# Experts of a two-block network: 256 gathers of key and value rows against panels of all keys and all values

## The reference

```python
def one_chunk(xt):                      # D = 1024, 8 heads, 128 x 128 = 16384 experts, top 16
    q = (xt @ w_q).reshape(BLOCK, PEER_HEADS, PEER_QDIM)
    s1 = jnp.einsum('chd,nd->chn', q[..., :half], keys1)
    s2 = jnp.einsum('chd,nd->chn', q[..., half:], keys2)
    t1, i1 = lax.top_k(s1, PEER_TOPK)
    t2, i2 = lax.top_k(s2, PEER_TOPK)
    cand = (t1[..., :, None] + t2[..., None, :]).reshape(BLOCK, PEER_HEADS, PEER_TOPK * PEER_TOPK)
    cidx = (i1[..., :, None] * PEER_NKEYS + i2[..., None, :]).reshape(...)
    ts, sel = lax.top_k(cand, PEER_TOPK)
    idx = jnp.take_along_axis(cidx, sel, axis=-1)
    g = jax.nn.softmax(ts, axis=-1)
    act = jax.nn.gelu(jnp.einsum('chkd,cd->chk', u[idx], xt))
    coef = (g * act).astype(xt.dtype)
    return jnp.einsum('chk,chkd->cd', coef, v[idx])
```

## Time and profile before

| | |
|---|---|
| time, median of 3 runs | 1437.83 us (1436.86 to 1438.47) |
| span of the profiled execution | 1437.5 us |
| PE busy | 1289.3 us, 90% of the span |
| DVE busy | 848.4 us, 59% |
| ACT busy | 422.1 us, 29% |
| POOL busy | 292.7 us, 20% |
| moved by DMA | 368 MB, a mean of 256 GB/s |
| mean granted clock of PE | 0.985 of full |

### The profile page before, as it was taken

One profiled execution on the slowest core, in us unless ns is written; L12 is line 12 of the kernel. 1 busy time (PEld: TensorE's weight loads), 2 busy tenths in 40 slices (PEclk: granted clock), 3 DMA queues, 4 the chain that ended last, 5 costly groups with the idle time before them and its releaser, 6 DMA issues.

```text
span 1437.5 us, 19206 instructions
## 1 busy us (share of the span) xinstructions
PE 1289.3 (90%) x7268; PEld 833.1 (58%) x7268; DVE 848.4 (59%) x2097; ACT 422.1 (29%) x974; POOL 292.7 (20%) x269
## 2 busy tenths in 40 slices
PE   7999998999999999999999989999877777777776
PEld 4446788986579878887888544444333332333322
DVE  7527866546563247232115867777777777777654
ACT  1215223121351136453003243333322322223212
POOL 0000000000000100000003344456543444444420
PEclk9999999999999999999999999999999999999999
DMA  9444100343324344432457999999999999999994
GB/s 308 158 151 133 33 3 3 118 146 117 118 89 151 110 136 148 127 106 88 146 209 297 421 421 403 421 421 421 421 421 421 421 421 420 422 421 420 422 422 202
DMA packets 68972, 367.98 MB, mean 256 GB/s; under 512 B 9295, under 2 KB 12751, under 8 KB 35793
## 3 DMA queue, kind: packets, MB, share of 16 engines
q0 software_dynamic: 37152, 269.50, 45.3%
q1 hardware_dynamic: 31586, 96.99, 20.4%
q10 hardware_dynamic: 144, 0.26, 0.0%
HBM read 365.67 MB, written 1.06 MB: 255 GB/s over the span
## 4 chain that ended last, share of the span: by engine, by line
PE 55%; DMA 24%; DVE 7%; ACT 2%; issue 1%; DVEq 0%; ACTq 0%
PE bank L1845 16%; PE bank L2491 11%; DMA arena<-peer_in,arena 7%; DMA row<-peer_in,arena 7%; DMA cst<-peer_in,arena 7%; PE bank L2437 3%; PE bank L1383 3%; DMA res<-peer_in,arena 2%; PE bank L1463 2%; PE bank L1440 2%; PE bank L805 2%; PE bank L614 1%; PE bank L604 1%; PE bank L1515 1%; PE bank L2425 1%
## 5 line engine op out<-in xcount | busy, mean ns | idle before, releaser
L2491 PE MATMUL bank<-arena 128*128 128x512 f32 x584 | 276.7, 614 | 65.1 <-ACT arena L2595 65.1
L2491 PEld LDWEIGHTS bank<-arena 128*128 128x128 f32 x584 | 109.1, 194 | 218.2 <-issue 217.9
L1845 PE MATMUL bank<-arena,ring 128*128 128x256 f32 (+2 forms) x1104 | 232.3, 371 | 2.2 <-DVE arena L2266 1.4
L1845 PEld LDWEIGHTS bank<-arena,ring 128*128 128x128 f32 x1104 | 198.8, 190 | 32.0 <-DVE arena L2266 1.8
L2732 DVE CUSTOM_DVE_ANT_0 arena<-arena 128x1024 f32<-128x1024 f32 x146 | 176.8, 1222 | 54.6 <-DMA arena<-peer_in,arena 54.4
L2777 POOL DMA_INDIRECT arena<-peer_in,arena x146 | 167.3, 1146 | 183.5 <-PE bank L2491 162.0
L2595 ACT ACTIVATE arena<-cst,arena 128x128 f32<-128x128 f32 x256 | 88.9, 394 | 133.8 <-DVE arena L2681 132.5
L2587 ACT ACTIVATE arena<-arena 128x2 f32<-128x2 f32 x129 | 38.0, 295 | 261.6 <-DVE arena L2732 261.5
L2491 PE MATMUL bank<-ring,arena 128*128 128x512 f32 x160 | 76.7, 623 | 21.7 <-ACT arena L2595 21.6
L2777 POOL DMA_INDIRECT row<-peer_in,arena x18 | 19.3, 1072 | 312.5 <-DVE arena L2669 276.3
L2491 PE MATMUL bank<-cst,arena 128*128 128x512 f32 x140 | 68.7, 624 | 13.6 <-ACT arena L2595 13.5
(11 more groups left out here) (400 smaller groups left out, 1982.1 us busy)
## 6 DMA issues: line engine op xcount, KB each, us to landing
ring<-stream_in SPq DMA_DIRECT2D x155, 512.0 KB, 3.6
ring<-stream_in SPq DMA_DIRECT2D x8, 384.0 KB, 6.5
arena<-stream_in SPq DMA_DIRECT2D x6, 512.0 KB, 7.2
arena<-peer_in,arena POOLq DMA_INDIRECT x146, 33.4
row<-rows_in SPq DMA_DIRECT2D x4, 512.0 KB, 18.7
cst<-cst_in SPq DMA_DIRECT2D x1, 1868.0 KB, 18.5
row<-rows_in POOLq DMA_DIRECT2D x2, 512.0 KB, 6.3
cst<-rg_w_in SPq DMA_DIRECT2D x1, 1024.0 KB, 7.9
```

The lines of the kernel that those rows point to most:

```text
L1845: mm = nc.tensor.matmul(bank[:, first:first + width], slot[:, at + k * cols:at + (k + 1) * cols], src[:, k, :], start=k == 0, stop=k == kt ...
L2491: mm = nc.tensor.matmul(core.banks[2 * t + b][:, :], diag[i % ND], value_half(i, b), start=False, stop=last)
```

## The change

No expert is gathered any more. The arrays u and v are brought in whole, as 128 panels each: panel j of the keys (`pu`) holds the experts whose second digit is j, 128 x 1024, and so does panel j of the values (`pv`). They come through the ring of `load_weights`, which has 4 places from then on instead of 8; the ring now takes panels in the order in which PE asks for them, and all transfers of SP are written at the end of the program.

PE meets all keys with all 256 normed tokens (`meet_keys`, 8 matmuls of 256 columns a panel). ACT takes the gelu of each pair of panels (`open_pair`) into an array G of 128 experts x 128 panels x 256 tokens. The routing stays on DVE, with its last steps on POOL (`decode`). PE turns the digits and weights so that choices lie on the partitions (`turn_picks`). For each token, POOL makes a matrix of 128 choices x 128 first digits that holds the weight where the digit fits (`make_ones`), DVE one of 128 choices x 128 second digits that holds ones, four tokens at once (`weigh_ones`), and PE multiplies the two: 128 x 128 weights for one token (`spread`, a group is four tokens, 64 groups). DVE multiplies these into the part of G that is there (`weave`), ACT copies the rest into G's part that is not there yet (`copy_rest`), and POOL multiplies the gelu of later panels onto it (`meet`). The spreads lie between the pairs of keys from pair 40 of 64 on, two or three groups after each pair. Then PE meets all values with G (`meet_values`, four matmuls of 512 columns a panel). The last projection of `second_mix` is made for 256 tokens at once there.

```diff
@@ -40,9 +40,7 @@
 DECAY = -float(np.exp(-0.5))
 SLOT = 1024
 RING = 8
-FIRST = 2
-EARLY = 7
-FIRST_AT = 17152
+LATE_RING = 4
...
-    out += [(("wq", m), SLOT) for m in range(EARLY, 2 * HP)]
+    out += [(("wq", m), SLOT) for m in range(2 * HP)]
+    out += [((name, j), D) for name in ("pu", "pv") for j in range(NK)]
...
+        elif key[0] == "pu":
+            m = tiles(w["peer_u_2"][0].reshape(NK, NK, D)[:, key[1]].T)
+        elif key[0] == "pv":
+            m = w["peer_v_2"][0].reshape(NK, NK, D)[:, key[1]]
...
+        if key not in self.slot_no:
+            place = self.next_place
+            self.next_place = (place + 1) % self.ring_places
+            self.place_count[place] += 1
+            self.came_before[key], self.in_place[place] = self.in_place[place], key
+            self.slot_no[key], self.slot_at[key] = len(self.slots), (place, self.place_count[place])
+            self.slots.append(key)
+        place, count = self.slot_at[key]
+        pe.wait_ge(self.slot_loaded[place], 16 * count)
+        return self.ring[place]
+    def shrink_ring(self):
+        self.ring_places, self.next_place = LATE_RING, 0
...
-            bank = claim(pe, ("mix", 0, m))
-            panel("mix", m, tiles(Y, T)[:, :, 0:P], KT, P, bank=bank).then_inc(*full(("mix", 0, m)))
+            panel("mix", m, tiles(Y, T), KT, T).then_inc(*full(("mix", m)))
+            core.used_by(("mix", m), ("mix", m))
...
+    UNITS = [(h, t) for h in range(HP) for t in range(TT)]
+    N, PAIRS = len(UNITS), NK // 2
+    QUAD, GROUPS, HELD = 4, T // 4, 3
+    WEAVE, LAST = 40, 4
...
+    def done_by(p):
+        return 0 if p < WEAVE else -(-(p + 1 - WEAVE) * GROUPS // (PAIRS - WEAVE))
+    def groups(p):
+        return range(done_by(p - 1), done_by(p))
+    pair_of = {q: p for p in range(PAIRS) for q in groups(p)}
...
+        def query(h):
+            key = ("wq", h)
+            bank = claim(pe, key)
+            for i in range(2):
+                slot = core.weights(pe, ("wq", 2 * h + i))
+                for k in range(KT):
+                    if h == 0 and i == 0:
+                        pe.wait_ge(g.gained.handle, k + 1)
+                    mm = nc.tensor.matmul(bank[:, i * T:(i + 1) * T], slot[:, k * P:(k + 1) * P], n2[:, k, :], start=k == 0, stop=k == KT - 1)
+                if i:
+                    mm.then_inc(*full(key))
+                    core.used_by(("wq", 2 * h + i), key)
+                else:
+                    mm.then_inc(*core.used_now(("wq", 2 * h + i)))
...
+        def meet_keys(j):
+            key = ("u", j // 2)
+            bank = core.banks[core.bank_at[key][0]] if j % 2 else claim(pe, key, 4 + j // 2 % 2)
+            slot = core.weights(pe, ("pu", j))
+            for k in range(KT):
+                mm = nc.tensor.matmul(bank[:, j % 2 * T:(j % 2 + 1) * T], slot[:, k * P:(k + 1) * P], normal[:, k, :], start=k == 0, stop=k == KT - 1)
+            if j % 2:
+                mm.then_inc(*full(key))
+                core.used_by(("pu", j), key)
+            else:
+                mm.then_inc(*core.used_now(("pu", j)))
...
+        def turn_picks(t):
+            key = ("picks", t)
+            bank = claim(pe, key, 6 + t)
+            pe.wait_ge(decoded.handle, N)
+            for i in range(2):
+                nc.tensor.transpose(bank[:, i * P:(i + 1) * P], index[:, i, t * P:(t + 1) * P], cst("ident"))
+            pe.wait_ge(weighed.handle, t + 1)
+            nc.tensor.transpose(bank[:, 2 * P:3 * P], weight[:, t * P:(t + 1) * P], cst("ident")).then_inc(*full(key))
...
+        def spread(q):
+            key = ("spread", q)
+            bank = claim(pe, key, 6 + q % 2)
+            pe.wait_ge(ones_weighed.handle, q + 1)
+            pe.wait_ge(ones_made.handle, q + 1)
+            for i in range(QUAD):
+                mm = nc.tensor.matmul(bank[:, i * NK:(i + 1) * NK], ONES[q % HELD][:, i, 0, :], ONES[q % HELD][:, i, 1, :], start=True, stop=True)
...
+        def meet_values(j, t):
+            slot = core.weights(pe, ("pv", j))
+            for b in range(2):
+                mm = nc.tensor.matmul(core.banks[2 * t + b][:, :], G[:, j, t * P:(t + 1) * P], half(slot, b), start=False, stop=j == NK - 1)
+                if j == NK - 1:
+                    mm.then_inc(*summed.up())
+            if t == TT - 1 and j < NK - 1:
+                mm.then_inc(*core.used_now(("pv", j)))
...
+        query(0)
+        core.shrink_ring()
+        g.ring_last = core.in_place[LATE_RING:]
+        sum_squares()
...
+        for h in range(2, HP):
+            query(h)
+            scores(h - 1)
+            if h == 2:
+                turn_factor()
+        scores(HP - 1)
+        pe.wait_ge(normed.handle, 1)
+        for p in range(PAIRS):
+            if p == WEAVE:
+                for t in range(TT):
+                    turn_picks(t)
+            for j in (2 * p, 2 * p + 1):
+                meet_keys(j)
+            for q in groups(p):
+                spread(q)
+        pe.wait_ge(woven.handle, GROUPS // 2)
+        for j in range(LAST):
+            meet_values(j, 0)
+        pe.wait_ge(woven.handle, GROUPS)
+        for j in range(LAST):
+            meet_values(j, 1)
+        pe.wait_ge(met.handle, PAIRS - WEAVE - 1)
+        for j in range(LAST, NK - LAST):
+            for t in range(TT):
+                meet_values(j, t)
...
-                for part in parts(n, q):
-                    act.wait_ge(dotted.handle, part.stop)
-                    nc.scalar.activation(act_out[:, part], dots[:, part], ACT.Gelu_apprx_tanh, scale=rstd[:, t:t + 1])\
-                      .then_inc(*activated.up())
-                    if q == 0 and 2 < n + 2 < N:
-                        scores(n + 2)
-                    act.wait_ge(coef_ready.handle, activated.count)
-                    for i in range(part.start, part.stop):
-                        if i >= ND:
-                            act.wait_ge(used.handle, i - ND + 1)
-                        nc.scalar.activation(diag[i % ND], cst("ident"), ACT.Copy, scale=act_out[:, i:i + 1])\
-                          .then_inc(*diag_ready.up())
...
+        def open_pair(p):
+            bank = filled(act, ("u", p))
+            before = done_by(p - 1) * QUAD
+            halves = tiles(bank[:, :], T)
+            if before:
+                n = p - WEAVE - 1
+                if n >= 2:
+                    act.wait_ge(met.handle, n - 1)
+                if n == 0:
+                    for key in g.ring_last:
+                        act.wait_ge(*core.slot_freed[key])
+                ins = nc.scalar.activation(tiles(spare[n % 2], T)[:, :, 0:before], halves[:, :, 0:before], ACT.Gelu_apprx_tanh)
+                ins.then_inc(*set_aside.up())
+            if before < T:
+                nc.scalar.activation(G[:, 2 * p:2 * p + 2, before:], halves[:, :, before:], ACT.Gelu_apprx_tanh).then_inc(*opened.up())
+                act.wait_ge(opened.handle, p + 1)
+            else:
+                act.wait_ge(set_aside.handle, set_aside.count)
+            act.sem_inc(*free(("u", p)))
+        def copy_rest(q):
+            bank = filled(act, ("spread", q))
+            first = 2 * (pair_of[q] + 1)
+            if first < NK:
+                by_key = bank[:, :].rearrange("p (t j) -> p j t", t=QUAD)
+                nc.scalar.activation(G[:, first:, tokens_of(q)], by_key[:, first:, :], ACT.Copy).then_inc(*rest_copied.up())
...
+        def weigh_ones(q):
+            if q < HELD:
+                for key in g.ring_last:
+                    dve.wait_ge(*core.slot_freed[key])
+            else:
+                filled(dve, ("spread", q - HELD))
+            copied(dve, ("picks", q * QUAD // P))
+            dve.wait_ge(laid.handle, q * QUAD // P + 1)
+            nc.vector.tensor_tensor(ONES[q % HELD][:, :, 1, :], index_t[:, tokens_of(q), 1:2].to_broadcast([P, QUAD, NK]),
+                                    cst("iota").unsqueeze(1).to_broadcast([P, QUAD, NK]), ALU.is_equal).then_inc(*ones_weighed.up())
+        def weave(q):
+            key = ("spread", q)
+            p = pair_of[q]
+            dve.wait_ge(opened.handle, min(p + 1, opened.count))
+            if rest_copied.count > q:
+                dve.wait_ge(rest_copied.handle, q + 1)
+            bank = filled(dve, key)
+            at = G[:, 0:2 * (p + 1), tokens_of(q)]
+            by_key = bank[:, :].rearrange("p (t j) -> p j t", t=QUAD)
+            nc.vector.tensor_tensor(at, at, by_key[:, 0:2 * (p + 1), :], ALU.mult).then_inc(*woven.up())
+            dve.wait_ge(woven.handle, q + 1)
+            dve.sem_inc(*free(key))
...
-                    for i in range(part.start, part.stop):
-                        arrived(dve, i)
-                        row = key_half(i)
-                        ins = nc.vector.tensor_tensor_reduce(out=row, in0=row, in1=half(X2, t), scale=1.0, scalar=0.0,
-                                                             op0=ALU.mult, op1=ALU.add, accum_out=dots[:, i:i + 1])
```

(50 more changed lines are left out.)

607 lines of the change are left out of this document (217 added, 390 removed).

## The result

The changed kernel takes 1805.67 us (median of 3, 1805.3 to 1808.13) against 1437.83 us before: 1.256 times as long, 95% interval 1.252 to 1.259. The profiled execution has a span of 1803.7 us; its own time is 1805.67 us. Every time given is the median of a kernel's fast runs: a single run of a single kernel, `e6_single_pass32` at 1455.05 us, was in the chip's slower state and is left out.

The account below looks back on a forecast made before the run. Gathers were taken to bound the experts stage before, PE the kernel after. From 737.5 us, 1039 us of PE work, 5.3 us to the end and 24 us of stall gave 1806 us (+25.6%), range 1780 to 1850.

Parts of the forecast that it names:

- The base: Start of the sum: PE's first matmul after the mixed rows, at 737.5 us.
- The 99 us of projection, queries and scores: PE work ahead of the keys, from last projection to turned picks: together 99 us.
- The keys: PE meeting 128 key panels: 2048 records of 256 columns at 0.216 us, 442 us.
- The values: PE meeting 128 value panels: 1024 records of 512 columns, 440 us, the same as the gathered form.
- The spreads and the stall: Weave, pairs 40 to 63: 58 us of outer products, plus PE idling about 1.5 us in 16 three-group pairs, 24 us.
- POOL's row: Weave: a weighted one-hot row of 128 columns takes POOL 0.22 us; POOL becomes the bound only at 0.8 us.
- POOL busy under a third: Sign expected in the profile after: POOL busy less than a third of the weave.
- rival (b): Weave worse through slow strided forms, slow POOL rows or a falling clock: 1851 us, or 1930 us; chance 0.25.
- The rule on the shared ports: Weave: one-hot blocks of DVE and POOL would alternate, 3 to 11 us more in all; left out of the sum.
- (c): Panel matmuls take one clock per column: 661 us go, end at 1145 us; chance 0.01.
- (a): Weave: the third group doesn't stall PE, 1782 us; chance 0.13.
- The claim on before: Experts stage of the kernel before: gathers bound it, 268 MB at 421 GB/s, 638 of 686 us.

Follow-up runs that it names:

- e6_single_pass32: Changed kernel with keys and values panels multiplied in float32r, panels rounded in place by ACT and DVE, and spreads begun at pair 32 instead of 40: 1444.68 us.
- e7_no_dve_ones: Changed kernel with DVE making its plain one-hot blocks for the first three groups only, 61 of 64 left out: 1793.87 us.
- e4_half_values: Changed kernel with values met for the first 512 of 1024 columns only, except in the last panel; all panels still brought in: 1595.16 us.
- e1_weave32: Changed kernel with spreads begun at pair 32 instead of 40, two groups in each of 32 pairs: 1782.67 us.
- e3_pool_half: Changed kernel with POOL making only two of the four one-hot rows of each group: 1801.88 us.
- e2_weave48: Changed kernel with spreads begun at pair 48 instead of 40, four groups in each of 16 pairs: 1846.15 us.
- b1_narrow_gathers: Kernel before, gathering 4 KB rows instead of 8 KB, keys alone, with the same number of gathers, rows and matmuls: 1357.9 us.
- e9_ring8_row4: As e8_ring8, with the fourth of each group's weighted one-hot rows made by DVE instead of POOL: 1309.44 us.
- e8_ring8: As e6_single_pass32, with eight ring places until three pairs before the spreads and again for the values: 1344.91 us.

## Why the prediction was right, point by point

**The base.** PE's first record of the projection started at 734.9 us, not 737.5. The two traces run within 0.2 us of each other for the first 150 us; from 120 to 240 us the mean clock was 0.97 before and 1.00 after, and the other kernels' traces have 736.1, 736.5, 737.1 and 737.2 there. The kernel after had gained its 2.5 us by 250 us, and from 160 to 200 us its mean granted clock was 1.00 and that of the others 0.87 to 0.96. But `e7_no_dve_ones` had 0.91 there and starts at 734.97 us, so the clock isn't all of it: it is scatter between executions of the same instructions, not the change.

**The 99 us of projection, queries and scores.** The first key panel starts at 832.37 us, 97.4 us on, and the picks, which the 99 us include, are turned in 0.65 us ahead of pair 40: six records, where I had counted twelve.

**The keys.** 442 us said. By starts the 80 panels before the weave took 276.3 us and each of the 24 pairs in it 6.91 us at the full clock, 442 us in all. The group's busy time is 448.1 us because the end of each row of records reaches 0.16 us into the first spread, and because of the low clock at 1121 to 1128 us. No idle time stands before it.

**The values.** 440 us said, 439.6 measured, and `e4_half_values` shows that they are worth that. This term carried the forecast: the dense form of the values costs PE what the gathered form did, so the keys and the spreads come on top.

**The spreads and the stall.** The values start at 1358.90 us, where I had 1360. PE idled 19.8 us, of which 15.5 behind DVE, 14 times at 1.1 us; I had 16 times 1.5. The chain was shorter by 0.4 us than I had it: the third group's spreads start 3.04 us after the first's, where I had 3.3, because ACT's two instructions for the pair overlap (0.66 us for both, not 0.77) and the hops are shorter, and PE's two spreads end at 1.95 us, not 1.8. That the weave cost nearly the 24 us anyway is luck: over its keys and spreads at full pace it took 26 us more, 19.8 of them idle, the rest the low clock after the wait for POOL and the ends of rows of records that idle time lays bare, neither of which is in my sum. The mechanism, the third block after the first weave, is shown three times: by `e1_weave32`, where it has no place, by `e3_pool_half`, where it stays with half of POOL's rows gone, and by `e7_no_dve_ones`, where the block isn't made. Strided reads of banks cost nothing extra: 0.52 us for 352 columns and 0.69 for 512 are the prices of the contiguous rows 7.

**What was mis-sized: POOL's row.** I took 0.22 us for a weighted one-hot row from a copy and a fill; it is 0.79 us by the median and 0.85 by the mean, about four times as much. The nearest rows, a fill and a copy, compare and multiply nothing, and said too little about it. I had put the point from which POOL decides at 0.8 us, and "POOL busy under a third" was wrong: it is busy 229 of 252 us. By my own threshold POOL would have been the bound. It cost 3.1 us of waits, 5 us with the clock behind them (`e3_pool_half`), because PE's pair with its stall took 10.2 us in the mean (10.9 us with three groups, from 1151.80 to 1162.72 us, and 8.7 with two), and POOL needed 10.7 x 0.85 + 0.7 = 9.8 us. The forecast was right here by 0.4 us a pair, which is luck. `e2_weave48`, with four groups a pair, shows what stands on the other side: 40 us more, with POOL as the bound and a low clock, which is rival (b)'s mechanism. The time that (b) gives for POOL at 1.5 us a row is wrong as it stands: 24 x 6.3 = 151 us come on top of 1806, 1957 us and not 1930.

**The rule on the shared ports.** The Trainium skill (SBUF — State Buffer, section "SBUF: two separate sides") has a DVE instruction with two SBUF inputs and a POOL instruction that reads SBUF block each other for a whole instruction. The runs agree that the two slow each other: with DVE's blocks POOL's rows take 852 ns, without them 799, and only rows that overlap a block are slow. They don't show a full block. In the changed kernel a row of POOL ran from 1153.74 to 1154.53 us and took 0.79 us as ever, while DVE's block of 1154.05 us took its 0.69 us; the next row took 0.90. In the mean a block of 0.69 us cost POOL 0.25 us ((939 - 790) x 107 / 64 ns), and apart from the very first row none took over 1.35 us. The price was on POOL, which had just room for it, and not 3 to 11 us on PE: DVE's blocks took 0.69 us by the median and 0.72 by the mean.

**The rivals.** (c) falls for float32: 2048 records of 216 ns for 1024 matmuls. For float32r it nearly is what happens: one record a matmul, 12 to 17% above one clock a column. (a) fell: the stall is there. That the transfers are hidden held: no wait of PE for a panel in the changed kernel.

**The claim on before.** `b1_narrow_gathers` shows that bytes bounded the experts stage, by 80 us over PE's work and waits.

**The step from span to time.** I had taken the timed run as 0.3 us above the profiled span. But the time of one and the same run lies 2 us above its span: 1805.67 and 1803.7 us here, and 1.7 to 3.1 us in all runs of the experiments.

**How near the number came.** 1806 against 1805.67 us is nearer than the mechanism earned. The base was 2.6 us too late and the terms ahead of the keys 0.9 us too long, while the weave took 2 us more than its terms and the step from span to time 1.7 us more. These cancel. What the runs confirm is each large term within 1 us, and the stall in kind, at 1.1 us instead of 1.5.

## What to carry to other kernels

Before a gather is replaced by the whole array, count what the engine beside the gathers has to do afterwards, at its own pace: here 638 us of transfers went, and PE, which had been busy 564 us beside them, was given 500 us of new work and was then busy 1027 us from 751.8 us on. Take a new instruction's price only from a row of its own kind; where none exists, work out from which price on it decides, and ask how far that is from the guess: here four times, and the guess was off by as much. And where an engine is nearly full, moving work off it can be paid back by what the other engine's instructions do to it (`e9_ring8_row4`: 58 us expected, 35 gained).

## What the runs showed of the hardware

- A weighted one-hot row of 128 columns (compare with a column's value, multiply by another) takes POOL 0.79 us, while DVE makes a plain block of 512 columns in 0.69 us.
- A float32r matmul leaves one record where float32 leaves two: 16 records of 256 columns took 2.14 us, so about 0.125 us each with the last one's end taken off, against 0.432 us in float32; 8 of 512 columns took 2.10 us, 0.24 us each, against 0.86. The granted clock was 1.00 in both stretches (859 to 870 and 1252 to 1259 us of `e8_ring8`), and at 2.4 GHz these are 300 clocks for 256 columns and 576 for 512, so 12 to 17% above one clock a column; the cause was not sought.
- The granted clock stayed at 1.00 from 1128.5 to 1359 us of the changed kernel, where PE idled 1.1 us in nearly every pair with three groups. It fell to a mean of 0.55 from 1121 to 1128 us, after idle times of 0.48 and 2.62 us with eight records between them, and to a mean of 0.90 in the weave of `e2_weave48`, where idle times of 0.5 to 2.7 us follow each other with eight records between them.
- A DVE instruction with both inputs in SBUF slows POOL's rows beside it (939 ns against 790 in the changed kernel); one that reads one input from a bank doesn't (795 ns in `e7_no_dve_ones`).
